# x first in the transfer queue, modulation pieces by pairs, two weight tiles multiplied by pairs of the contraction

## The reference, cut to what matters

```python
mod = jnp.einsum('bd,de->be', c, w_mod[l]) + b_mod[l]
sh1, sc1, gt1, sh2, sc2, gt2 = jnp.split(mod, N_MOD, axis=-1)

h = modulate(rmsnorm(x, norm1_g[l]), sh1, sc1)
z = jnp.einsum('bsd,de->bse', h, w_in[l])
...
u_pool = z[..., o:o + POOL_W]; o += POOL_W
```

## Time and profile before

| | |
|---|---|
| median of three runs | 2185.13 us (2184.76 to 2185.3) |
| span of the profiled execution | 2183.5 us, 1.6 us under the median of the runs |
| PE busy in the span | 2135.9 us, 98% |
| DVE, ACT busy | 1591.9 us (73%), 1297.9 us (59%) |
| the stretch 0 to 50.28 us (until the last product of tile 3) | PE busy 35.96 us |
| the stretch 50.28 to 100 us | PE busy 49.72 us of 49.72 |

### The profile page before, as it was taken

One profiled execution on the slowest core, in us unless ns is written; L12 is line 12 of the kernel. 1 busy time (PEld: TensorE's weight loads), 2 busy tenths in 40 slices (PEclk: granted clock), 3 DMA queues, 4 the chain that ended last, 5 costly groups with the idle time before them and its releaser, 6 DMA issues.

```text
span 2183.5 us, 36554 instructions
## 1 busy us (share of the span) xinstructions
PE 2135.9 (98%) x13700; PEld 1904.0 (87%) x13700; DVE 1591.9 (73%) x3503; ACT 1297.9 (59%) x2442; POOL 100.4 (5%) x136
## 2 busy tenths in 40 slices
PE   7999999999999999999999998999999999999998
PEld 5988888888999988888889988888899998888886
DVE  3455659898888767888866655798988887555556
ACT  3355545666999754445545544565679986555554
POOL 0000000303000000000000000013030000000000
PEclk9999999999999999999989999999999999999999
DMA  8665566665444467778744634666654445566664
GB/s 334 203 210 180 178 184 185 200 185 183 136 127 127 155 202 284 282 276 289 257 145 135 204 97 129 187 189 194 192 172 127 126 127 174 182 194 193 194 194 133
DMA packets 110495, 407.42 MB, mean 187 GB/s; under 512 B 11504, under 2 KB 11888, under 8 KB 110064
## 3 DMA queue, kind: packets, MB, share of 16 engines
q1 hardware_dynamic: 98880, 361.81, 53.1%
q10 hardware_dynamic: 11440, 43.28, 5.1%
HBM read 403.99 MB, written 1.05 MB: 185 GB/s over the span
## 4 chain that ended last, share of the span: by engine, by line
PE 93%; DVE 3%; ACT 2%; issue 1%; POOL 1%; DMA 0%; ACTq 0%; DVEq 0%
PE PB L477 20%; PE PB L479 20%; PE PB L478 20%; PE PB L889 11%; PE PB L887 6%; PE PB L861 6%; PE PB L812 2%; PE PB L886 2%; PE PB L544 1%; PE PB L811 1%; PE PB L828 1%; PE PB L558 1%; PE PB L523 1%; POOL AR L2346 1%; DMA X<-in_x 0%
## 5 line engine op out<-in xcount | busy, mean ns | idle before, releaser
L1639 DVE TENSOR_TENSOR WL<-RING,WH 128x1024 fp32r<-128x1024 f32 x651 | 801.9, 1233 | 444.2 <-ACT WH L1182 442.1
L1182 ACT ACTIVATE WH<-RING 128x1024 fp32r<-128x1024 f32 x651 | 686.7, 1055 | 438.7 <-PE PB L479 430.9
L477 PE MATMUL PB<-WH,HX 128*128 128x512 f32 (+2 forms) x1344 | 494.4, 368 | 7.2 <-DVE HX L1694 3.3
L479 PE MATMUL PB<-WH,HX 128*128 128x512 f32 (+2 forms) x1344 | 490.5, 365 | 0.0
L478 PE MATMUL PB<-WL,HX 128*128 128x512 f32 (+2 forms) x1344 | 490.1, 365 | 0.0
L477 PE MATMUL PB<-HX,WH 128*128 128x256 f32 x1440 | 424.6, 295 | 6.8 <-DVE HX L1694 6.0
L479 PE MATMUL PB<-HX,WL 128*128 128x256 f32 x1440 | 409.4, 284 | 0.0
L478 PE MATMUL PB<-HX,WH 128*128 128x256 f32 x1440 | 409.1, 284 | 0.0
L889 PE MATMUL PB<-HX,WH 128*128 128x512 f32 x1092 | 389.1, 396 | 0.0
L887 PE MATMUL PB<-HX,WL 128*128 128x256 f32 x1248 | 322.4, 279 | 0.0
L477 PEld LDWEIGHTS PB<-WH,HX 128*128 128x128 f32 x1344 | 255.3, 190 | 51.4 <-issue 4.9
(11 more groups left out here) (239 smaller groups left out, 2075.7 us busy)
## 6 DMA issues: line engine op xcount, KB each, us to landing
RING<-in_u SPq DMA_DIRECT2D x256, 512.0 KB, 3.7
RING<-in_v SPq DMA_DIRECT2D x256, 512.0 KB, 4.2
RING<-in_win SPq DMA_DIRECT2D x90, 512.0 KB, 3.9
AR<-in_wm ACTq DMA_DIRECT2D x40, 1024.0 KB, 6.5
RING<-in_wq SPq DMA_DIRECT2D x32, 512.0 KB, 3.7
AR<-in_wm SPq DMA_DIRECT2D x8, 1024.0 KB, 16.3
RING<-in_wout SPq DMA_DIRECT2D x16, 512.0 KB, 3.6
RING<-in_sk SPq DMA_DIRECT2D x8, 512.0 KB, 3.6
```

Source lines behind the costliest of these rows:

```text
L477: e.matmul(o, ah, bh, start=start, stop=False)
L479: return e.matmul(o, al, bh, start=False, stop=stop)
L1182: e.activation(hi(t), raw(("w", t), words(t)), ACT.Copy).then_inc(s_hi, 1)
L1639: e.tensor_tensor(lo(t), raw(("w", t), words(t)), hi(t).bitcast(F32), ALU.subtract).then_inc(s_lo, 1)
```

## The change

Transfers: x moves from ACT's queue to the head of SP's; the pieces go as 0, 1, tiles 0, 1, pieces 2 to 7, tiles 2, 3; the constants `C1` go behind tile 7 (`W_Q + 2`) in place of tile 4. PE: the transposes go between pieces 0 and 1; `pool_in(c, kp)` now does one pair of the contraction, 12 matmuls, for both token halves; the pairs of tiles 0 and 1 are set between the pieces, and tiles 2 and 3 run by pairs at the end. ACT and DVE: the norm goes ahead of piece 0's copy; tiles 0 and 1 are both split after pair 0, and tile 2 only after pair 3. PSUM: pieces 0 and 1 use banks 1 and 2, all others bank 3 (the products of the two column halves use banks 1 and 2 from the first pair on).

```diff
--- before.py
+++ after.py
@@ -414,7 +414,7 @@
 
         def chunk_sums(g):
 
-            b, o = (1 + g % 3, 0) if g < 4 else (3, 0) if g < N_START else (2 + g % 2, 0) if 20 <= g < 24 else (0, 256)
+            b, o = (1 + min(g, 2), 0) if g < N_START else (2 + g % 2, 0) if 20 <= g < 24 else (0, 256)
             return PB[b], o, MR0[:, g, :] if g < N_START else MR[:, g % 2, :] if g < LATE else MRV[:, g - LATE, :]
 
         def chunk_source(g):
@@ -430,11 +430,12 @@
                     return wpool
                 return (sk2 if i >= 4 else sk1)[i % 2]
 
-            def first_chunks(g0):
-                for g in range(g0, g0 + 4):
+            def first_chunks(g0, g1):
+                for g in range(g0, g1):
                     e.dma_start(chunk(g), chunk_source(g)).then_inc(chunk_landed(g)[0], 16)
 
-            first_chunks(0)
+            e.dma_start(X[:, :, :], x.rearrange("(a p) d -> p a d", p=128)).then_inc(s_x, 16)
+            first_chunks(0, 2)
             for f, (kind, i) in enumerate(PLAN):
                 if f >= NSLOT:
                     was, n = PLAN[f - NSLOT]
@@ -447,8 +448,8 @@
                 n = words(i) if kind == "w" else SLOTW
                 e.dma_start(raw((kind, i), n), source(kind, i)).then_inc(s_slot[f % NSLOT], 16)
                 if (kind, i) == ("w", 1):
-                    first_chunks(4)
-                if (kind, i) == ("w", W_F):
+                    first_chunks(2, N_START)
+                if (kind, i) == ("w", W_Q + 2):
                     e.dma_start(C1, consts[:, K_P1:K_P1 + N_P1]).then_inc(s_band, 16)
                 if (kind, i) == ("w", W_V + 6):
                     e.wait_ge(s_ah, 4)
@@ -531,7 +532,7 @@
                 e.wait_ge(*chunk_landed(g))
                 if g < N_START:
                     if g >= 3:
-                        e.wait_ge(s_mev, g if g >= 4 else 1)
+                        e.wait_ge(s_mev, g)
                 else:
                     e.wait_ge(s_mev, g - 1 if 21 <= g < 24 else g)
                     if g == 20:
@@ -567,47 +568,50 @@
                         r = e.matmul(PB[b][:, 128 * k:128 * k + 128], ones, DG[:, kk % 2, :], start=True, stop=True)
                         r.then_inc(s_bp, 1)
 
-            def pool_in(c, u):
-
-
+            def pool_in(c, kp):
+
+
+                u = kp // 2
                 n = W_POOLIN + 2 * u + c
                 wh, wl = (t.rearrange("p (k n) -> p k n", k=4) for t in (hi(n), lo(n)))
                 tile_ready(e, n)
+                e.wait_ge(s_hl, kp + 1)
                 for a in range(2):
                     tok = slice(128 * a, 128 * a + 128)
-                    for k in range(4):
-                        kk = 4 * u + k
-                        if kk % 2 == 0:
-                            e.wait_ge(s_hl, kk // 2 + 1)
-                        r = three(PB[1 + c][:, 256 * a:256 * a + 256], HH[:, kk, tok], HL[:, kk, tok], wh[:, k, :],
-                                  wl[:, k, :], (a, kk) == (0, 0), (a, kk) == (1, KT - 1))
-                r.then_inc(s_used, 1)
+                    for kk in (2 * kp, 2 * kp + 1):
+                        r = three(PB[1 + c][:, 256 * a:256 * a + 256], HH[:, kk, tok], HL[:, kk, tok],
+                                  wh[:, kk - 4 * u, :], wl[:, kk - 4 * u, :], (a, kk) == (0, 0), (a, kk) == (1, KT - 1))
+                if kp % 2:
+                    r.then_inc(s_used, 1)
 
 
             mod_chunk(0)
+            e.wait_ge(s_kc, 16)
+            transposed(0)
             mod_chunk(1)
-            e.wait_ge(s_kc, 16)
             columns(0)
             columns(1)
-            transposed(0)
+            pool_in(0, 0)
             mod_chunk(2)
+            pool_in(1, 0)
             mod_chunk(3)
             columns(2)
             columns(3)
             mod_chunk(4)
-            pool_in(0, 0)
+            pool_in(0, 1)
             mod_chunk(5)
             columns(4)
             columns(5)
+            pool_in(1, 1)
             mod_chunk(6)
-            pool_in(1, 0)
             columns(6)
             mod_chunk(7)
             columns(7)
 
 
-            pool_in(0, 1)
-            pool_in(1, 1)
+            for kp in (2, 3):
+                pool_in(0, kp)
+                pool_in(1, kp)
             wh, wl = (t.rearrange("p (k n) -> p k n", k=KT) for t in (hi(W_F), lo(W_F)))
             tile_ready(e, W_F)
             for a in range(2):
@@ -1261,28 +1265,25 @@
                     copy(BC[:, 512 * h:512 * h + 512], PB[banks[h]][:, :], s_bc)
 
             e.dma_start(SM[:, :], smalls).then_inc(s_small, 16)
-            e.dma_start(X[:, :, :], x.rearrange("(a p) d -> p a d", p=128)).then_inc(s_x, 16)
             e.dma_start(KC[:, :], consts[:, 0:N_KC]).then_inc(s_kc, 16)
             e.wait_ge(s_small, 16)
             e.activation(SM[:, C_C2:C_C2 + 8], SM[:, C_C2:C_C2 + 8], ACT.Silu).then_inc(s_silu, 1)
             e.activation(ST[:, 47:48], SM[:, 0:1], ACT.Sqrt, scale=0.0)
-            chunk_out(0)
             e.wait_ge(s_x, 16)
             square(X[:, 1, :], 1, 0, 1024).then_inc(s_sq, 1)
             root(0)
             scaled(XN, X, 0, 31)
+            chunk_out(0)
             chunk_out(1)
             norm_part(0, 0, 0, 0, 0)
+            fill(0, 2)
             chunk_out(2)
             chunk_out(3)
-            fill(0, 1)
             norm_part(0, 1, 0, 0, 0)
-            fill(0, 2)
             chunk_out(4)
             chunk_out(5)
             norm_part(0, 2, 0, 0, 0)
             chunk_out(6)
-            fill(0, 3)
             chunk_out(7)
             norm_part(0, 3, 0, 0, 0)
 
@@ -1719,8 +1720,8 @@
                     e.wait_ge(s_gs, kp + 1)
                     turned(kp)
                     low(kp)
-                    if kp < 3:
-                        fill(0, kp + 1)
+                    if kp == 0:
+                        fill(0, 2)
 
             def bcast(i0, col):
                 for kk in range(8):
```

## The result

The changed kernel is slower: median 2191.06 us of 6 runs (2189.63 to 2193.17) against 2184.91 us of 6 runs before (2182.99 to 2185.3), ratio 1.0032 with the 95% interval 1.0022 to 1.0042. Between the medians that is +6.1 us; the span of the profiled execution went from 2183.5 to 2189.2 us, +5.7. The forecast was +4.5 us with a range that holds the result, but it gave the larger chance to "within 0.2%" (0.51), and that was wrong: the interval lies over 0.2%.

What follows compares the result with a forecast made beforehand. TensorE was taken as the bound, busy 98% of the span, so only its early gaps and clock could move. Terms -4.2 + 2.6 + 3.5 + 1.6 + 1.0 gave +4.5 us, 2189.6 us; range 2184.5 to 2191.7.

Steps and rivals of the forecast that it cites:

- within 0.2%: Verdict class for the whole kernel: measured time less than 0.2%, 4.4 us, from the kernel before; chance 0.51.
- To the first product: Start-up until tile 0 is split: x lands at 6.1 us, first product at 20.6 instead of 24.85, gaining 4.2 us.
- The rounds: First product to last pair's difference: pieces now stand behind products, losing 2.6 us, plus 3.5 us for the clock.
- The two terms: From first product to last difference: 2.6 us for the new order, 3.5 us for half rate from two gaps.
- Tile 2: Behind the last pair chain: tile 2's split now starts there, so TensorE waits 1.6 us more.
- Transfers at nothing: Piece transfers: last piece lands again at 31.1 us, wanted at 36.3 at the earliest, so no cost.
- The last 48 products and what follows: Behind the last gap: products again 7.8 us, plus 1 us for this and piece 8; ends -2 and +2.4.
- The 7.79 us: Window 42.49 to 50.28 of the kernel before, taken as the price of the last 48 products, 6.1 us at half rate.
- the 4.4 us line: Whole kernel: 0.2%, the smallest difference a measurement can tell from no change; the +4.5 us sum sits on it.
- The arrival of the pieces as the limit: Rival: TensorE keeps up with the transfers, piece 7 is multiplied on landing at 31.1; 2179.9 us, chance 0.08.
- One fall less: Rival: pair chain 1's gap brings no half rate, 1.6 us less; +1 to +3, about 2187.1 us, chance 0.22.
- half rate in every round: Rival: waits between runs of 12 products double piece and product work from 20.6 us on; +8, 2193 us, chance 0.12.

Runs made afterwards that it cites:

- e3: Changed kernel with pieces 2, 3 and 4 put ahead of tile 0's products, 5 and 6 ahead of tile 1's; 2187.52 us, ratio 1.0016 to before.
- e5: Changed kernel with 19 useless matmuls filling TensorE's gaps, every wait kept; 2188.62 us, ratio 1.0015 to before.
- e2: Changed kernel with tile 2 split early again, after pair 2, between the copies of pieces 6 and 7; 2189.00 us, ratio 1.0019 to before.
- e7: e1 with 6 useless matmuls, 4 ahead of piece 4 and 2 behind columns 7; 2180.68 us, ratio 0.9980 to before.
- e1: Kernel before with only x moved to the head of SP's queue, its norm and transposes earlier; 2182.15 us, ratio 0.9990 to before.
- e10: Kernel before with the run of 48 narrow matmuls broken up, 24 between tile 3's products, 24 behind piece 8; 2182.84 us, ratio 0.9987 to before.
- e6: e1 with tile 0's pairs on either side of piece 4 and tile 1's second pair behind columns 7; 2179.36 us, ratio 0.9978 to before.
- e8: Changed kernel with the edits of e3 and e2 together; 2185.67 us, ratio 1.0006 to before.
- e9: e6 with the run of 48 narrow matmuls broken up, 24 between tile 3's products, 24 behind piece 8; 2178.06 us, ratio 0.9969 to before.

## Why the prediction was right or wrong, by its steps

- **To the first product: right.** Predicted at 20.6, measured at 20.61. x landed by 6.11 (predicted 6.1). That the end is right to 0.01 us is partly luck: piece 0 was 0.5 us later than predicted (9.22), and the transposes (3.25 us for 3.52) and piece 1 (1.00 for 1.2) made it good.
- **The rounds: right in mechanism, 0.4 us short.** From there to the last difference 17.6 + 2.6 + 3.5 = 23.7 us were predicted, 24.1 measured (20.61 to 44.72). e3 supports the cause. The two terms don't split it as their names say, though. The 17.6 us of before hold 3.4 us at half rate, which cost 1.7, while the 20.2 of the new rounds were summed at full rate. At full rate it is 15.9 before and 24.1 - 3.4 = 20.7 after: of the 6.5 us, 4.8 are order and 1.7 are clock. The two half-rate stretches came where they were put, at the first product and at pair chain 1, and e5 confirms that the gaps bring them.
- **Tile 2: right for the changed kernel**, 1.5 us against 1.6. e2 shows what a repair would meet: with tile 2 early, tile 3's split ends the wait.
- **Transfers at nothing: right.** The last piece was issued at 11.5, took 19.6 and landed at 31.1, as predicted; TensorE took it at 40.05.
- **The last 48 products and what follows: this step failed.** It was put at +1.0 us, for these products and piece 8, the middle between no change and half of one more stretch; the narrow run between them and the q products behind them stood at nothing. Measured: +0.34 on the products (8.13 against 7.79), +1.13 on the narrow run with piece 8 (8.56 against 7.43), and +0.47 from there to the mark (199.96 us against 199.49), where the q products are still at half rate until 65.15. Together 1.9, and most of it where nothing was put. Piece 8 itself gave nothing (1.87 against 1.86, at half rate both times); the narrow run gave 1.12, 6.69 against 5.57. e5 and e7 show that the narrow run takes 8.16 and 8.08 us when most of it is at half rate, against 5.57 in before and 5.69 in e1, and e10 that it brings a fall itself.
- **The 7.79 us were misread.** They were taken as 48 products, but their row counts 43 matmuls: six of tile 2's products ran beside the last pair chain, and 42 were left. In the changed kernel all 48 stand behind the gap. Six more cost 0.7 us at full rate; that the row grew by only 0.34 is because less of it was at half, 5.2 us against 6.1. The two errors hid each other. The first and the last of the six, before:

```profile
39.74 0.36 PE L477 MATMUL PB<-WH,HX 128*128 128x256 f32 x1
...
40.41 0.28 PE L479 MATMUL PB<-WH,HX 128*128 128x256 f32 x1
```

- **The chances: wrong.** The sum was put on the 4.4 us line and half of its case on each side, with nothing for the fact that all omitted terms were of one sign: each new fall was given the 3.4 us of the shortest one in the rows, and the work behind the 48 products was left out. 0.4 and 0.9 us on top make 5.8, and the likeliest class was the wrong one.
- **The rivals.** The arrival of the pieces as the limit (faster) did not happen in the change, where TensorE takes piece 7 nine microseconds after it lands; in part it does in e1, e3 and e6, where the pieces stand ahead of products and TensorE waits for some of them. One fall less did not happen in the profile.
- **The rule of the Trainium skill** (TensorE: Matmul & The Clock Gate, section HAM oscillation), to run a tile's contraction in one go because waits between short groups throw the clock back: the trace of the change agrees as far as the gaps go, with 0.60 in and 0.82 behind the first of its two gaps of 4 us, 0.80 in and 0.68 behind the second. Yet the rival's size, half rate in every round, did not come: the 12 products of tile 1 from 24.84 on and the 12 from 36.41 on ran at full rate, 0.12 us apart. But e6 cuts two tiles by pairs and has no fall before 46 us. The waits between the groups matter, not the cut.

What stays open: which fall makes the distance between a profile and the median of its kernel. That it goes with the clock is on record, where each run has its mean granted clock beside its time: e3's seven runs near 2188.1 us had 0.988 and its two near 2184.9 had 0.991; e5's three near 2184.0 had 0.993 and the others 0.991 to 0.992. It would take several profiles of one kernel to say how often each fall comes. Three parts of the change were not tried apart: pieces 2 to 7 behind tiles 0 and 1 in the queue (e8 keeps it, with one wait of 2.06 us for a piece, and lies some 3.5 us over e1, with intervals that just overlap), the place of the C1 table, and the single PSUM bank for pieces 2 to 7.

## What to carry to other kernels

In a start-up where a short serial chain on other engines (here 2.5 us per pair) follows each transferred piece, put the piece that feeds the next chain ahead of any bulk work, and keep the bulk work that is already ready to stand beside the chain; the change here did the reverse, and from the first product to the last pair's difference that cost 6.5 us, 4.8 by order and 1.7 by the clock. Price an idle gap on TensorE as the gap plus half of the half-rate stretch behind it, and look for such a stretch behind a run of narrow matmuls too. When a row is carried over as a price, count the instructions in it. When a sum lands on the line between two verdicts, look which way its omitted terms point.

## What the runs showed of the hardware

- Inside a run of 48 matmuls with 16 columns, with TensorE busy 100% in the profile, the granted clock fell to 1.2 GHz in all ten profiles that have it (0.64 over 49.14 to 57.30 in e5, where all before had 1.00), and at that rate they went at 0.21 us each in place of 0.11. With 24 of them singly between wide products and 24 behind piece 8 there was no fall in e10; in e9 there was one at 50.1, behind the last of them.
- 19 matmuls that compute nothing, put where TensorE would wait anyway, saved about 3.7 us of 2191 in the changed kernel, by the ratios and by the mark (e5; the two intervals just overlap).
- At the very start the granted clock in the rows is 1.00 while the durations are those of half rate: 16 strip matmuls take 1.94 us at 9.22 and 1.07 at 14.33 in the changed kernel. For this stretch the durations tell the clock, the column doesn't.
